# Fourteen modulation parts in each round of the recurrence, none in the output stage and the first norm, and length spreads from rounded halves

## The chip, the cores and the metric

The kernel runs as one program on one core of a Trainium2 chip. A core has TensorE (PE: matmuls, with its weight loads shown as PEld), VectorE (DVE), ScalarE (ACT), GpSimd (POOL) and SyncE (SP, which here only issues DMAs). Each engine works through its own queue in order; semaphores order the queues against each other. The metric is the time of one execution on the device in microseconds (us); smaller is better. Starts of instructions are counted from the beginning of the profiled span.

## The reference

Two blocks are computed one after the other in fp32 for 256 tokens x and 256 context tokens, width 1024. The first is a mixing layer with a gated delta rule in both directions and a pooling branch, the second two layers of feed-forward, mixer (short convolution, then latent attention) and feed-forward. Every norm is scaled and shifted by vectors that a large matrix makes of a condition, the modulation:

```python
def adaln_chunks(cond, w_mod, b_mod):
    m = jax.nn.silu(cond) @ w_mod + b_mod          # [1, 9*D] for each layer
    return jnp.split(m[:, None, :], N_MOD, axis=-1)

# first block
q, k = _l2_norm(q), _l2_norm(k)                    # of 8 heads, 128 wide
o_f, s_f = _gated_delta_rule(q, k, v, g[0], beta[0], s0_f)        # chunks of 64 tokens, forward
o_b, s_b = _gated_delta_rule(flip(q), flip(k), flip(v), ...)      # backward
x = x + gate_x * jnp.einsum('blm,md->bld', y_x, w_out[layer])     # y_x: both mixers, 2048 wide
x = _rms_norm(x, final_gain)
# second block, for x and for ctx
h = h + 0.5 * m[2] * swiglu(rms_norm(h, g) * (1 + m[1]) + m[0])
h = h + m[5] * short_conv_mixer(...) or latent attention
h = h + 0.5 * m[8] * swiglu(...)
```

## The kernel before, in words

**Stages.** The kernel goes through an input stage (0 to about 256 us), the recurrence (256 to about 512), the output stage (to 579), and then the second block: feed-forward 0, short convolution (from about 995), feed-forward 1 and 2, latent attention and feed-forward 3. It is one long queue for TensorE with the other engines around it.

**Dense products.** A weight arrives as a chunk of 128 x 1024 fp32 (`w_raw`, issued by SP). ACT rounds it to fp32r (`w_hi`, L901), POOL makes the rest (`w_lo`, L584), and TensorE multiplies three times for each tile: low weights by high data (L620), high by high (L621), high by low (L624). POOL's wait is for ACT's `w_hi`, TensorE's for POOL's `w_lo`. Four chunks are in flight.

**Modulation parts.** The modulation matrix is streamed as parts of 512 KB, 16 to a group of 2048 columns. A part costs TensorE four matmuls of 512 columns (`mod_part`, L664), it waits for its DMA, and its buffer goes back to SP when it is done. Two parts side by side are what the slots below call a pair; their products run on different rows of the result. When a group is complete, ACT copies the bank to `mod_row` (`act_mod_copy`, L688), TensorE turns it with four transposes (`mod_turn`, L674), and DVE adds the bias (`dve_mod_bias`). The first part of the next group waits for the copy. Parts of the recurrence live in a ring of six buffers (`RECUR_RING`: three `mod_raw`, three `w_raw` that the dense stages don't need at that time), later ones in a ring of nine (`late`).

**The recurrence.** There are eight rounds (`ROUNDS`: four steps, two halves of the heads), each for both directions. `inverse(r)` inverts a triangular matrix by blocks: `left` (L1679) and `right` (L1690) alternate with copies on ACT and products on DVE, then a level of 32-blocks (L1789, L1791), a level of 64-blocks (L1801) and its last product (L1811). Then come the gram and the sums of the next round (L1595, L1605) and the new values (L1713); the state is updated in L1658. ACT makes the decay of a round (`decay`, L1850 and an exponential, L1854), and the copies of each level (L1866, L1875, L1910 to L1930). DVE makes `first_blocks` and `masked_gram` and the products between levels. `some_mods(r, slot)` puts modulation parts at four places of TensorE's queue in each round: "first" (behind the first `left` and `right`), "half" (between the 32-blocks and L1801), "last" (between L1801 and L1811) and "key" (at the end of the round). A copy or a turn of a group is placed at the slot in which the group ends or the next has begun. Before the first `left` of round 0 TensorE runs filler matmuls, `keep_busy(4)`, 512 columns by two each (L722).

**Lengths of keys and queries.** In the input stage, the squares of q and k are summed, DVE and ACT make of them 128 rows `rk` (64 rows `rq`), one row for a head and a quarter of the tokens, with ACT's square root (L1247, L1248). `spread_lengths` (L1130) spreads a row over 128 partitions by four fp32 matmuls whose weights are a broadcast column of the identity; each compiles to two. There are 12 of these calls (8 for keys, 4 for two query heads each), placed between dense products, and DVE multiplies by the result.

**Output stage and first norm.** The output product goes over 16 chunks; parts stand before chunk tiles 10 and 12 (`LATE_OUT`), behind the product and before the spread of the norm (`LATE_END`), and in the first norm of feed-forward 0 (`LATE_TURNS`). SP's loads for them are interleaved with the chunks. A norm is: square sums (L740), a reciprocal root by DVE and ACT, its spread (L759), and the scaled tokens, whose `n_hi` (L866) the first dense product needs. Group 7's copy stands in `act_ffn`, its turn at the start of the short convolution.

## Time and profile before

| | |
|---|---|
| median of 3 runs | 2247.94 us (2246.88 to 2253.41) |
| profiled execution | 2247.81 us |
| its span in the trace | 2246.0 us |
| TensorE busy | 2192.4 us, 98% |
| VectorE, ScalarE, GpSimd busy | 37%, 35%, 45% |
| granted TensorE clock, mean | 0.995 |
| data read from HBM | 294 MB, 132 GB/s |

The profiled execution lies 1.8 us above its own span, which is what a run has around the first and the last recorded instruction. The profile is read by place: a stage's row on the timeline of an engine gives start, time, line and what it works on, "x8" stands for eight instructions merged in one row (start of the first, time from there to the end of the last), and the brackets at the end of a row give the idle time before it and what ended it. Neighbouring matmuls overlap in the rows, since their ends are modelled; the distance between starts is what an instruction costs TensorE's queue. The mean clock is not 1 because of a few short stretches at half rate.

### The profile page before, as it was taken

How to read it: one execution, taken by the hardware profiler on the slowest of the kernel's cores; microseconds unless marked ns; L12 is line 12 of the kernel's file. 1: busy time of each engine (PE TensorE's matmuls, PEld its weight loads, DVE VectorE, ACT ScalarE, POOL GpSimd, SP SyncE). 2: the span in 40 equal slices, each digit the busy share in tenths (PEclk: the TensorE clock that was granted, in tenths of full speed). 3: DMA queues.
4: the chain of work that ended last, by engine and by line, in shares of the span. 5: the costliest groups of instructions: out<-in, count | busy, mean ns of one | idle time of the engine just before them, and what ended most of it. 6: DMA issues, size and time to landing. Idle time of an engine off the chain costs nothing.

```text
span 2246.0 us, 36868 instructions
## 1 busy us (share of the span) xinstructions
PE 2192.4 (98%) x14756; PEld 1789.6 (80%) x14756; DVE 841.6 (37%) x1512; ACT 780.3 (35%) x1259; POOL 1012.4 (45%) x469
## 2 busy tenths in 40 slices
PE   7999999989999999999999999999999999999999
PEld 5789777768788888878878888887888887759999
DVE  4667566665511311343471131133122113562212
ACT  4445434434422122132232212213222222554444
POOL 0457523245344444434434444443444444306888
PEclk9999999999999999999999999999999999999999
DMA  8335466447353323324324323332433323304566
GB/s 288 103 114 162 169 220 223 170 171 276 119 169 94 94 93 94 97 79 172 94 85 163 100 94 94 94 94 90 163 94 94 94 94 118 124 20 124 186 188 188
DMA packets 90932, 297.56 MB, mean 132 GB/s; under 512 B 8992, under 2 KB 21664, under 8 KB 90400
## 3 DMA queue, kind: packets, MB, share of 16 engines
q1 hardware_dynamic: 90640, 295.05, 40.2%
q8 instruction: 117, 1.92, 0.4%
q10 hardware_dynamic: 144, 0.34, 0.1%
q14 instruction: 31, 0.25, 0.0%
HBM read 294.31 MB, written 1.05 MB: 132 GB/s over the span
## 4 chain that ended last, share of the span: by engine, by line
PE 76%; issue 12%; POOL 6%; DVE 3%; ACT 1%; DMA 1%; SPq 1%; POOLq 0%; DVEq 0%; ACTq 0%
PE bank L620 22%; PE bank L624 22%; PE bank L621 22%; POOL w_lo L584 5%; PE bank L664 2%; PE bank L1679 1%; PE bank L1690 1%; DVE gdn_outer L2048 1%; PE bank L1658 1%; PE bank L1595 1%; DMA first_mods<-in_modstream 1%; PE bank L1130 0%; DVE gdn_outer L2050 0%; PE bank L1702 0%; DMA mod_raw<-in_modstream 0%
## 5 line engine op out<-in xcount | busy, mean ns | idle before, releaser
L584 POOL TENSOR_TENSOR w_lo<-w_raw,w_hi 128x1024 fp32r<-128x1024 f32 x378 | 918.9, 2435 | 1054.7 <-ACT w_hi L901 1054.0
L620 PE MATMUL bank<-n_hi,w_lo 128*128 128x512 f32 (+1 forms) x2220 | 788.8, 355 | 5.2 <-ACT n_hi L974 1.8
L624 PE MATMUL bank<-n_lo,w_hi 128*128 128x512 f32 (+1 forms) x2220 | 781.2, 352 | 0.1
L621 PE MATMUL bank<-n_hi,w_hi 128*128 128x512 f32 (+1 forms) x2220 | 781.1, 352 | 0.0
L901 ACT CAST w_hi<-w_raw 128x1024 fp32r<-128x1024 f32 x382 | 400.3, 1050 | 760.5 <-PE bank L624 737.7
L620 PEld LDWEIGHTS bank<-n_hi,w_lo 128*128 128x128 f32 x2220 | 417.6, 188 | 80.3 <-issue 15.4
L624 PEld LDWEIGHTS bank<-n_lo,w_hi 128*128 128x128 f32 x2220 | 417.5, 188 | 64.6 <-DVE n_lo L806 0.6
L621 PEld LDWEIGHTS bank<-n_hi,w_hi 128*128 128x128 f32 x2220 | 417.7, 188 | 62.7
L2461 DVE TENSOR_TENSOR prod<-silu,bank 128x512 f32<-128x512 f32 (+1 forms) x88 | 54.6, 621 | 709.2 <-PE bank L624 692.8
L620 PE MATMUL bank<-g_hi,w_lo 128*128 128x512 f32 (+1 forms) x768 | 283.2, 369 | 1.4 <-DVE g_lo L2452 1.4
L621 PE MATMUL bank<-g_hi,w_hi 128*128 128x512 f32 (+1 forms) x768 | 282.9, 368 | 0.0
L624 PE MATMUL bank<-g_lo,w_hi 128*128 128x512 f32 (+1 forms) x768 | 282.9, 368 | 0.0
L2420 DVE SCALAR_TENSOR_TENSOR h<-bank,gates,h 128x256 f32<-128x256 f32 x136 | 60.7, 480 | 312.8 <-PE bank L624 312.8
L620 PEld LDWEIGHTS bank<-g_hi,w_lo 128*128 128x128 f32 x768 | 144.0, 188 | 28.9 <-DVE g_lo L2452 1.8
L624 PEld LDWEIGHTS bank<-g_lo,w_hi 128*128 128x128 f32 x768 | 144.0, 188 | 27.3
L621 PEld LDWEIGHTS bank<-g_hi,w_hi 128*128 128x128 f32 x768 | 144.0, 188 | 27.2
L2406 ACT ACTIVATE silu<-bank 128x512 f32<-128x512 f32 (+1 forms) x88 | 48.0, 545 | 288.3 <-PE bank L624 288.3
L2452 DVE TENSOR_TENSOR g_lo<-prod,g_hi 128x512 fp32r<-128x512 f32 (+1 forms) x88 | 84.5, 962 | 1.9 <-ACT g_hi L2396 1.9
L1339 DVE SCALAR_TENSOR_TENSOR conv<-bank,cols,conv 128x508 f32<-128x508 f32 (+3 forms) x96 | 63.0, 659 | 42.3 <-ACT conv L1279 39.7
L1980 POOL TENSOR_TENSOR gdn_t<-gdn_inner,consts 128x256 f32<-128x256 f32 x16 | 11.7, 730 | 137.1 <-DVE gdn_inner L2033 137.1
L881 DVE TENSOR_TENSOR nt<-h 128x512 f32<-128x512 f32 (+1 forms) x56 | 58.6, 1047 | 1.8
L866 ACT ACTIVATE n_hi<-nt,mods 128x256 fp32r<-128x256 f32 x88 | 41.0, 505 | 41.8 <-DVE nt L821 41.8
(395 smaller groups left out, 1868.1 us busy)
## 6 DMA issues: line engine op xcount, KB each, us to landing
w_raw<-in_stream SPq DMA_DIRECT2D x383, 512.0 KB, 3.6
late<-in_modstream SPq DMA_DIRECT2D x56, 512.0 KB, 4.6
mod_raw<-in_modstream SPq DMA_DIRECT2D x48, 512.0 KB, 6.3
w_raw<-in_modstream SPq DMA_DIRECT2D x48, 512.0 KB, 5.4
first_mods<-in_modstream SPq DMA_DIRECT2D x6, 1024.0 KB, 11.6
h<-in_tokens SPq DMA_DIRECT2D x2, 1024.0 KB, 6.2
first_mods<-in_modstream SPq DMA_DIRECT2D x4, 512.0 KB, 8.9
consts<-in_consts SPq DMA_DIRECT2D x1, 1152.0 KB, 5.9
```

What stands on the lines that cost most here:

```text
L584: nc.gpsimd.tensor_tensor(w_lo[:, slot, :], w_raw[:, slot, :], w_hi[:, slot, :].bitcast(F32), ALU.subtract).then_inc(w_lo_ready, 1)
L620: nc.tensor.matmul(out_ap, wl, hi, start=start, stop=False)
L621: nc.tensor.matmul(out_ap, wh, hi, start=False, stop=False)
L624: return nc.tensor.matmul(out_ap, wh, lo, start=False, stop=stop)
L664: last = nc.tensor.matmul(bank[MOD_BANK][32 * j:32 * j + 32, :], cond[:, which, k, :], room[:, jj * 512:(jj + 1) * 512], start=(k == 0), s ...
L881: square = nc.vector.tensor_tensor(nt[:, k % 2, s_], h[:, k, s_], h[:, k, s_], ALU.mult)
L901: nc.scalar.copy(w_hi[:, c % RING, :], w_raw[:, c % RING, :]).then_inc(w_hi_ready, 1)
L1339: ins = nc.vector.scalar_tensor_tensor(acc[:, :, to], src[:, :, of], col(Cols.CONV + ci * CONV + j), acc[:, :, to], ALU.mult, ALU.add)
L2406: nc.scalar.activation(silu[:, f % 2, 0:w], bank[(g0 + g) % BANKS][:, 0:w], ACT.Silu).then_inc(gate_ready, 1)
L2420: last = nc.vector.scalar_tensor_tensor(h[:, d, s_], bank[g % BANKS][:, s_], gates[:, gate, d, c:c + 1], h[:, d, s_], ALU.mult, ALU.add)
L2452: nc.vector.tensor_tensor(g_lo[:, f, 0:w], prod[:, f % 2, 0:w], g_hi[:, f, 0:w].bitcast(F32), ALU.subtract).then_inc(hid_lo, 1)
L2461: nc.vector.tensor_tensor(prod[:, f % 2, 0:w], silu[:, f % 2, 0:w], bank[g % BANKS][:, 0:w], ALU.mult).then_inc(groups_read, 2)
```

## The change

`MOD_ROUND` goes from 12 to 14, with 2, 4, 2 and 6 parts in the slots "first", "half", "last" and "key" in place of 2, 2, 4 and 4. The 16 parts of the output stage and of the first norm are no longer there, nor are SP's loads for them, and group 7 is copied and turned within the recurrence. The place of the other copies and turns follows from the counts. The lengths are spread as a rounded half and a rest in fp32r, from rows that ACT lays out for each quarter (12 operations with a scale of zero or one), with the rest made by POOL in front of chunk `TAIL + 8`; a key spread is two matmuls of 512 columns, a query spread four of 256. The value transposes, gates and rate use the modulation bank and the query sums the other one, so that waits move. ACT passes over the pooled groups without waiting for them, one filler matmul is left of four, and DVE makes the first blocks of the forward direction ahead of the backward gram. Three lines with the same bank exchange are cut here.

```diff
@@ -70,7 +70,7 @@
-MOD_ROUND = 12
+MOD_ROUND = 14
 RECUR_RING, LATE_RING = 6, 9
@@ -81,9 +81,9 @@
-LATE_OUT = {10: 2, 12: 2}
-LATE_END = (4, 4)
-LATE_TURNS = {("ffn", 0): (0, 0, 4, None), ("sc", 0): (4, 2, 2, None), ("ffn", 1): (4, 2, 2, 8), ("ffn", 2): (4, 2, 2, None),
+LATE_OUT = {}
+LATE_END = (0, 0)
+LATE_TURNS = {("ffn", 0): (0, 0, 0, None), ("sc", 0): (4, 2, 2, None), ("ffn", 1): (4, 2, 2, 8), ("ffn", 2): (4, 2, 2, None),
               ("mla", 0): (4, 2, 2, 9)}
@@ -321,6 +321,13 @@
             rq = s2("rq", [2 * 32, P])
+            k_rows = s2("k_rows", [P, 4, P])
+            k_rows_hi = s2("k_rows_hi", [P, 4, P], F32R)
+            k_rows_lo = s2("k_rows_lo", [P, 4, P], F32R)
+            q_rows_hi = s2("q_rows_hi", [2 * 32, 2, P], F32R)
+            q_rows_lo = s2("q_rows_lo", [2 * 32, 2, P], F32R)
+            of_quarter = s2("of_quarter", [P, 4])
+            head_rows = s2("head_rows", [P, 32], F32R)
             decay_rate = s2("decay_rate", [16, 16])
@@ -535,21 +542,8 @@
         sp.wait_ge(d_o, 8)
-        for q in range(7):
-            load_late(sp, q)
-        stream_loads(sp, IN_LOADS + RING, CH_OUT + 12)
-        sp.wait_ge(y_lo_ready, 8)
-        for q in (7, 8):
-            load_late(sp, q)
-        q = LATE_RING
-        for i in range(12, 16):
-            load_late(sp, q)
-            q += 1
-            stream_loads(sp, CH_OUT + i, CH_OUT + i + 1)
-        stream_loads(sp, CH_OUT + 16, CH_FFN[0] + RING)
-        for q in range(q, MOD_PARTS):
-            load_late(sp, q)
-        q = MOD_PARTS
+        stream_loads(sp, IN_LOADS + RING, CH_FFN[0] + RING)
+        q = 0
@@ -596,7 +590,11 @@
             low_half(pool, i, i % RING)
-        low_halves(pool, 2 * RING, N_IN)
+        lengths_at = TAIL + 8
+        assert lengths_at % RING == 0
+        low_halves(pool, 2 * RING, lengths_at)
+        pool_lengths(pool)
+        low_halves(pool, lengths_at, N_IN)
         low_half(pool, N_IN, N_IN % RING)
@@ -1087,13 +1085,13 @@
         for t in range(4):
-            last = nc.tensor.transpose(bank[MISC_BANK][:, t * 64:(t + 1) * 64], gb[:, t * P:(t + 1) * P],
+            last = nc.tensor.transpose(bank[MOD_BANK][:, t * 64:(t + 1) * 64], gb[:, t * P:(t + 1) * P],
                                        C(Const.IDENT, 64)[:, 0:64])
...
         pe.wait_ge(rate_diag, 1)
-        nc.tensor.matmul(bank[MISC_BANK][:, 256:272], C(Const.ONES, 16), decay_rate[:], start=True, stop=True)\
+        nc.tensor.matmul(bank[MOD_BANK][:, 256:272], C(Const.ONES, 16), decay_rate[:], start=True, stop=True)\
             .then_inc(rate_rows, 1)
@@ -1115,21 +1113,28 @@
+    q_rows = act_out[0:2 * 32, 0, 0:2 * P].rearrange("p (t c) -> p t c", t=2)
+
+    def pool_lengths(pool):
+        pool.wait_ge(kq_rstd, 3)
+        nc.gpsimd.tensor_tensor(k_rows_lo[:], k_rows[:], k_rows_hi[:].bitcast(F32), ALU.subtract).then_inc(kq_rstd, 1)
+        nc.gpsimd.tensor_tensor(q_rows_lo[:], q_rows, q_rows_hi[:].bitcast(F32), ALU.subtract).then_inc(kq_rstd, 1)
+
     def spread_lengths(pe, j):
...
         if j == 0:
-            pe.wait_ge(kq_rstd, 1)
+            pe.wait_ge(kq_rstd, 5)
             pe.wait_ge(gb_tok_ready, 1)
...
             pe.wait_ge(kq_scaled, j - 1)
-        for t in range(4):
-            q, head, rows = (t, hd, rk) if kind == "k" else (t % 2, hd + t // 2, rq)
-            n = rows.shape[0]
-            last = nc.tensor.matmul(bank[kq_bank(j)][:, t * P:(t + 1) * P],
-                                    C(Const.IDENT, n)[:, 32 * q + head:32 * q + head + 1].to_broadcast([n, P]),
-                                    rows[:], start=True, stop=True)
+        for e, (hi, lo) in enumerate([(k_rows_hi, k_rows_lo)] if kind == "k" else [(q_rows_hi, q_rows_lo)] * 2):
+            n, width = hi.shape[0], hi.shape[1] * P
+            room = bank[kq_bank(j)][:, e * width:(e + 1) * width]
+            head = head_rows[0:n, hd + e:hd + e + 1].to_broadcast([n, P])
+            nc.tensor.matmul(room, head, hi[:].rearrange("p t c -> p (t c)"), start=True, stop=False)
+            last = nc.tensor.matmul(room, head, lo[:].rearrange("p t c -> p (t c)"), start=False, stop=True)
         last.then_inc(kq_bc, 1)
@@ -1153,17 +1158,17 @@
                 pe.wait_ge(silu_done, ci + 1)
-                if ci == 8:
-                    pe.wait_ge(sums_read, 1)
-                else:
+                if ci > 8:
                     pe.wait_ge(vtok_done, ci - 8)
                 for t in range(4):
-                    last = nc.tensor.transpose(bank[MISC_BANK][:, t * P:(t + 1) * P],
+                    last = nc.tensor.transpose(bank[MOD_BANK][:, t * P:(t + 1) * P],
                                                act_out[:, ci % 2, t * P:(t + 1) * P], C(Const.IDENT))
...
                 pe.wait_ge(tile_sq, ci + 1 if ci < 8 else ci - 7)
-                b = MISC_BANK if ci < 8 else MOD_BANK
+                if ci == 16:
+                    pe.wait_ge(sums_read, 1)
+                b = MISC_BANK
                 tiles = w // P
@@ -1244,8 +1249,16 @@
             act.wait_ge(kq_ms, 2)
-            nc.scalar.activation(rk[:], rk[:], ACT.Sqrt)
+            nc.scalar.activation(rk[:], rk[:], ACT.Sqrt).then_inc(kq_rstd, 1)
             nc.scalar.activation(rq[:], rq[:], ACT.Sqrt).then_inc(kq_rstd, 1)
+            act.wait_ge(kq_rstd, 2)
+            for t in range(4):
+                for room in (k_rows, k_rows_hi):
+                    nc.scalar.activation(room[:, t], rk[:], ACT.Identity, scale=of_quarter[:, t:t + 1])
+            for t in range(2):
+                for room in (q_rows, q_rows_hi):
+                    last = nc.scalar.activation(room[:, t], rq[:], ACT.Identity, scale=of_quarter[0:2 * 32, t:t + 1])
+            last.then_inc(kq_rstd, 1)
@@ -1266,6 +1279,8 @@
             for g in groups:
+                if g >= TAIL and IN_TAIL_GROUPS[g - TAIL][0] == "pool":
+                    continue
                 act.wait_ge(linear_done, done_in(g))
@@ -1292,8 +1307,6 @@
                     continue
-                if kind == "pool":
-                    continue
                 if n and IN_TAIL[n - 1][0] == "u":
@@ -1315,17 +1328,21 @@
         nc.vector.memset(row_sum[:], 0.0).then_inc(pads_clear, 1)
+        ident = C(Const.IDENT)
+        nc.vector.tensor_reduce(of_quarter[:], ident.rearrange("p (t h) -> p t h", t=4), AX_X, ALU.add)
+        step(nc.vector.tensor_reduce(k_rows[:, 0, 0:32], ident.rearrange("p (t h) -> p h t", t=4), AX_X, ALU.add))
+        step(nc.vector.tensor_copy(head_rows[:], k_rows[:, 0, 0:32]))
...
             dve.wait_ge(gb_turned, 1)
-            step(nc.vector.tensor_copy(gb_tok[:].rearrange("p t r -> p (t r)"), bank[MISC_BANK][:, 0:256]))
+            step(nc.vector.tensor_copy(gb_tok[:].rearrange("p t r -> p (t r)"), bank[MOD_BANK][:, 0:256]))
             nc.vector.scalar_tensor_tensor(tot[:], gb_tok[:, :, 0:16], -1.0, gb_tok[:, :, 0:16],
...
             nc.vector.tensor_copy(v_tok[:, :, vi, :],
-                                  bank[MISC_BANK][:].rearrange("p (t d) -> p t d", t=4)).then_inc(vtok_done, 1)
+                                  bank[MOD_BANK][:].rearrange("p (t d) -> p t d", t=4)).then_inc(vtok_done, 1)
@@ -1396,7 +1413,7 @@
             dve.wait_ge(tile_used, 24)
-            nc.vector.tensor_scalar(rq[:], bank[MOD_BANK][0:2 * 32, 0:P], EPS, float(P), ALU.add, ALU.mult)\
+            nc.vector.tensor_scalar(rq[:], bank[MISC_BANK][0:2 * 32, 0:P], EPS, float(P), ALU.add, ALU.mult)\
                 .then_inc(sums_read, 1)
@@ -1498,7 +1515,7 @@
-    MOD_SLOTS = {"first": 2, "half": 2, "last": 4, "key": 4}
+    MOD_SLOTS = {"first": 2, "half": 4, "last": 2, "key": 6}
     mod_copies, mod_turns = {}, {}
@@ -1721,7 +1738,7 @@
                 pe.wait_ge(kq_scaled, len(KQ_ITEMS) - 1)
-                keep_busy(4, MISC_BANK)
+                keep_busy(1, MISC_BANK)
             left(r, 1, FWD)
@@ -2081,9 +2098,9 @@
+        first_blocks(0, FWD)
         masked_gram(dve, 0, BWD)
-        for d in (FWD, BWD):
-            first_blocks(0, d)
+        first_blocks(0, BWD)
         for r, (step_, hg) in enumerate(ROUNDS):
@@ -2388,8 +2405,6 @@
         act_norm(act, i, m, w, LATE_TURNS.get(("ffn", n), (None,))[-1])
-        if n == 0:
-            act_mod_copy(act, RECUR_LAST + 1)
         for half in range(2):
@@ -2476,8 +2491,6 @@
         def before_in(g, k):
-            if g == SC_FIRST and k == 0:
-                mod_turn(pe, RECUR_LAST + 1)
             return operands(g, k)
@@ -2519,8 +2532,6 @@
         dve_norm(dve, "sc", i, m, T)
-        dve_mod_bias(dve, RECUR_LAST + 1)
-        dve.wait_ge(mod_ready, MOD_BLOCKS + RECUR_LAST + 1)
         step(dve_gate(dve, 3))
```

## Rows read from the trace of the kernel before

**Rows 1.** The page, busy time of each engine: us, share of the span, instructions.

```profile
PE 2192.4 (98%) x14756; PEld 1789.6 (80%) x14756; DVE 841.6 (37%) x1512; ACT 780.3 (35%) x1259; POOL 1012.4 (45%) x469
```

**Rows 2.** Timeline of ACT, 180 to 184: start us, us, engine, line, operation.

```profile
182.13 0.29 ACT L1248 ACTIVATE rq<-rq 64x128 f32<-64x128 f32 x1
182.33 1.03 ACT L901 CAST w_hi<-w_raw 128x1024 fp32r<-128x1024 f32 x1
```

**Rows 3.** Timeline of ACT, 248 to 262.

```profile
255.08 1.15 ACT L1850 ACTIVATE gdn_dec<-bank,neg_cum 128x128 f32<-128x128 f32 x4 [4.77 <-PE bank L624]
```

**Rows 4.** Timeline of POOL, 183 to 190.

```profile
183.44 7.11 POOL L584 TENSOR_TENSOR w_lo<-w_raw,w_hi 128x1024 fp32r<-128x1024 f32 x3 [2.23 <-ACT w_hi L901]
```

**Rows 5.** Timeline of PE, 185.4 to 186.2.

```profile
185.99 0.35 PE L620 MATMUL bank<-n_hi,w_lo 128*128 128x256 f32 x1 [0.40 <-POOL w_lo L584]
```

**Rows 6.** Two windows: us; busy PE, PEld, DVE, ACT, POOL; PE clock, DMA share, GB/s.

```profile
1945.00:1948.00 3.00, 0.94 (x6) 0.71 (x5) 2.23 (x1) 1.48 (x3) 3.00 (x2) 1.00 0.25 101
1948.00:1951.00 3.00, 3.00 (x9) 2.31 (x9) 2.76 (x6) 1.70 (x4) 1.46 (x1) 0.52 0.64 209
```

**Rows 7.** Timeline of PE, 232 to 238, a key and a query spread.

```profile
232.72 1.05 PE L1130 MATMUL bank<-rk,consts 128*128 128x128 f32 x8
233.53 0.36 PE L620 MATMUL bank<-n_hi,w_lo 128*128 128x256 f32 x1
...
236.56 1.16 PE L1130 MATMUL bank<-rq,consts 64*128 64x128 f32 x8
237.64 0.39 PE L620 MATMUL bank<-n_hi,w_lo 128*128 128x256 f32 x1
```

**Rows 8.** Timeline of PE, 251.5 to 266, the start of the recurrence.

```profile
251.50 1.05 PE L1595 MATMUL bank<-consts,gb_tok 128*128 128x128 f32 x8
...
257.73 3.70 PE L722 MATMUL bank<-consts 128*128 128x512 f32 x8
```

**Rows 9.** Timeline of PE, 335.9 to 345.4, the second half of a round.

```profile
336.66 0.96 PE L1801 MATMUL bank<-gdn_outer,gdn_a 64*64 64x64 f32 x16 [0.66 <-DVE gdn_outer L2134]
337.55 1.07 PE L664 MATMUL bank<-w_raw,cond 128*32 128x512 f32 x8
...
339.41 0.96 PE L1811 MATMUL bank<-gdn_t,gdn_outer 64*64 64x64 f32 x16
```

**Rows 10.** Timeline of ACT, 333.6 to 341, the copy of a group.

```profile
339.57 0.59 ACT L688 COPY mod_row<-bank 128x512 f32<-128x512 f32 x1 [1.47 <-PE bank L664]
```

**Rows 11.** Timeline of PE, 287.3 to 293.7, and from 375.3 to 382.

```profile
288.39 0.62 PE L664 MATMUL bank<-mod_raw,cond 128*32 128x512 f32 x2
...
292.56 1.06 PE L664 MATMUL bank<-mod_raw,cond 128*32 128x512 f32 x8
...
378.57 0.68 PE L1679 MATMUL bank<-gdn_outer,gdn_inner 64*64 64x64 f32 x16 [1.26 <-ACT v_tok L1875]
```

**Rows 12.** SP's loads of modulation parts (L459), 345.3 to 345.95, and their landing.

```profile
L459 SPq DMA_DIRECT2D w_raw<-in_modstream x1: 425/425/425, 345.8 to 345.8; - x1
...
DMA to landing us min/median/max: 3.7/4.2/4.6
```

**Rows 13.** Timeline of PE, 544.9 to 547, the output stage.

```profile
544.97 0.28 PE L624 MATMUL bank<-n_lo,w_hi 128*128 128x256 f32 x1
...
546.17 0.39 PE L620 MATMUL bank<-n_hi,w_lo 128*128 128x256 f32 x1
```

**Rows 14.** Timeline of PE, 578.9 to 590.2, the first norm.

```profile
579.04 3.64 PE L664 MATMUL bank<-late,cond 128*32 128x512 f32 x16
...
589.81 0.50 PE L620 MATMUL bank<-n_hi,w_lo 128*128 128x512 f32 x1
```

**Rows 15.** Timeline of ACT, 579 to 590, the second square.

```profile
579.99 0.49 ACT L2268 ACTIVATE kT<-h,cols 128x256 f32<-128x256 f32 x1
```

**Rows 16.** Timeline of PE, 606.3 to 607.6, feed-forward 0.

```profile
607.19 0.50 PE L620 MATMUL bank<-n_hi,w_lo 128*128 128x512 f32 x1 [0.31 <-POOL w_lo L584]
```

**Rows 17.** Timeline of PE, 994.9 to 996, start of the short convolution.

```profile
995.23 0.60 PE L674 MATMUL bank<-consts,mod_row 128*128 128x128 f32 x4
```

2 lines of the change are left out of this document (1 added, 1 removed).

## The prediction

> **What bounds the kernel now.** I read four views in this order. The page's busy times say that TensorE is busy for 98% of the span and no other engine for half of it [rows 1], so an edit counts where it adds to or takes from TensorE's own queue, or where TensorE waits. The timeline of PE around each edited line then says whether an instruction starts straight behind the one before it (TensorE's own time) or stands behind an idle time with a releaser. The timelines of ACT and POOL at the same moments say what is late next. The landings of SP's loads, last, say when a modulation part can be used at the earliest. TensorE's clock reads 1.0 almost everywhere; the exceptions matter below.
>
> **The change, part by part.** Times are those of the profiled execution, 2247.8 us beside a span of 2246.0; the median is 0.1 us above it, so sum and median can be compared directly.
>
> (a) *Lengths in the input stage.* ACT gets twelve 128-column operations behind the square root of L1248. The one there is followed 0.20 us later by the next [rows 2]; four of L1850 take 1.15, so 0.29 each [rows 3]. Twelve cost 2.4 to 3.4 us, I take 3.0. Behind them on ACT stands the w_hi of chunk 32 (L901), behind that POOL's w_lo (2.37 each) [rows 4], and TensorE already waits 0.40 us for exactly this chunk at 185.99 [rows 5]. No cover: +3.0. POOL's two subtractions (half and a quarter of the columns of an L584: 1.2 and 0.6) stand in front of chunk 33's low half; chunk 33 is ready 1.8 + 2.4 = 4.2 us after chunk 32, TensorE wants it after some 3.3, which is 24 matmuls and the running sums: +0.85. TensorE is then idle for about 3.4 us in one piece. A comparable hole, busy for 0.94 of 3.00 us, is followed by a granted clock of 0.52, which is 1.2 GHz [rows 6]. Three microseconds of it cost half, 1.5 to 1.7, of which 0.85 only takes the place of the wait for chunk 33: +0.85. (Trainium skill, "TensorE: Matmul & The Clock Gate", Part 1: without activity the array falls back to half rate. This trace agrees, and the rule speaks against the change; without it this part would be 0.85 less.)
>
> (b) *The spreads.* A key spread holds TensorE from 232.72 to 233.53, 0.81 us, a query spread from 236.56 to 237.64, 1.08 [rows 7]. The new form streams 1024 columns of fp32r; 24 matmuls of 256 take 3.03 us in the same rows, 0.12 each, so 1024 columns cost 0.48 to 0.5. For the queries, whose weights have 64 rows, the extra 0.27 may stay. No row has this form, so I bound it: 8 x 0.31 and 4 x (0.1 to 0.6) give 2.8 to 4.9, less what goes where TensorE then waits for DVE's scaling; taken 3.7. (a) and (b) together: 3.0 + 0.85 + 0.85 - 3.7 = **+1.0**. The swap of banks 6 and 7 for values, gates and sums removes waits that nobody feels; DVE's three setup operations lie in an idle time of DVE. Nothing for both.
>
> (c) *Start of the recurrence.* ACT's first decay (L1850) starts at 255.08 after 4.77 us idle, released by the last pooled matmul [rows 3], which the new `continue` no longer awaits. Its input, the sums of L1595, is there at 251.50 + 1.05 = 252.6 [rows 8], so the forward decay comes 2.5 us earlier. Now the order counts: DVE does the forward blocks while the backward gram is still being made. ACT's queue (backward decay, cast, three exponentials, the copy of L1875) then sets the first L1679, some 1.8 us earlier than now. The filler matmuls end at 261.43 [rows 8]; with one instead of four (0.93 each) they end at 258.7 and cover nothing that is late. **-1.8**.
>
> (d) *Two more parts in each round.* Four parts take TensorE from 337.55 to 339.41 [rows 9]: 0.93 a pair. Eight pairs are 7.4 us; one more turned group in the recurrence (L674) 0.6. New group ends now fall in the middle of a slot: parts 47|48 (round 2, "half"), 95|96 and 111|112 (rounds 5 and 6, "key"). There part p waits for ACT's copy, 0.59 [rows 10] and two semaphores, about 0.75 each: 2.25. Sum 10.3. What hides it: in "half", L1801 waits 0.66 for DVE (L2134) [rows 9], in five rounds of steps 1 to 3, and 0.1 in round 4: 3.4; in "last" nothing, the pair taken out there is a full gain, counted in the sum; in "key", L1679 waits 1.26 us in round 3 [rows 11], 0.22 in round 1, and the output stage 0.93: 2.4. Left: **+4.5**. Behind the key slot wait left, right and "first" of the next round, all TensorE's own queue.
>
> (e) *The ring of six.* In the old order the two parts of "first" use buffers freed in "last", 10 us before. With six parts in "key" they use those freed by the first pair of "key". That pair starts at K = 288.39, "first" at 292.56 [rows 11], K + 4.2; with one pair more about K + 5.15. Two loads issued behind such a pair (the second at 345.8, the first 0.4 before it, for K = 344.36 [rows 9]) land after 3.7 and 4.6 us [rows 12], so at K + 4.8 and K + 6.1. The second part is 0.95 late, and as both parts run side by side, the lateness is paid in full. Round borders 0, 1, 2, 3, 4 pay 0.85 to 1.0, borders 5 and 6, stretched by a copy and a turn, some 0.2 each: **+5.0**, bounds 0 (other engines' chain is the later one) and 6.5.
>
> (f) *Output stage.* Between the matmuls at 544.97 and 546.17 two parts cost 1.20 - 0.12 = 1.08 us [rows 13]. Two such places: **-2.2**. Twelve loads less on SP's queue there bring chunks earlier, for which TensorE did not wait. The longer "key" slot of round 7 ends with y_lo: nothing.
>
> (g) *First norm.* Four parts run from 579.04 for 3.64 us, twice their price: the clock is low [rows 14]. ACT's last square ends at 580.48 [rows 15], so the sums come 2.1 us earlier; the second and third four give another 1.3 where they outlast the chain on DVE and ACT. TensorE's first matmul moves from 589.81 [rows 14] to about 586.4. But nothing is left that raises the clock before it: 1.4 to 3.1 us of the dense matmuls' time is lost at half rate, 2.2 taken. TensorE's wait at 607.19 for w_lo [rows 16] goes, as ACT comes 3.6 us earlier (3.0 and the copy). -3.4 - 0.3 + 2.2, rounded down for the slower spreads: **-1.6**, bounds -3.3 and 0.
>
> (h) *Short convolution.* The turn at 995.23 goes [rows 17]: **-0.4**.
>
> Sum: 1.0 - 1.8 + 4.5 + 5.0 - 2.2 - 1.6 - 0.4 = +4.5, so 2252.3 us.
>
> **Rivals.** *The landing costs nothing*: (e) is zero since the chains on DVE and ACT end later than the load. For it: DVE works through first blocks of the other direction at that time. Against it: at 292.56 TensorE starts without idle time. 2247.3 us. *Everything moved is hidden*: (d) and (e) are zero and (g) reaches its bound; 2247.8 + 1.0 - 1.8 - 2.2 - 3.3 - 0.4 = 2241.1 us. Against it: the key slots of rounds 0, 2, 4, 5 and 6 have no gap. *The clock falls in the recurrence (slower)*: place: behind the single filler, where TensorE has 1.2 us idle and then halves of a round with 0.4 us holes; the three fillers taken out covered that. Price: half of each low microsecond; 6.8 us low give +3.4, 15 us +7.5, so 2255.7 to 2259.8, middle 2257.5. It decides once low stretches beyond those in my sum pass 4.5 us. For it: the granted clock after [rows 6]; against it: the whole recurrence now runs at 2.4 GHz with holes up to 1.26 us [rows 11]. (The page's rule named above gives this rival too.) *The change doesn't do what it says*: rounded spreads take as long as before; +3.7, 2256.0 us.
>
> **How the numbers follow.** Forecast 0.44, landing free 0.20, all hidden 0.10, clock 0.22, spreads 0.04. A measurement of this kernel can tell about 0.3%, 6.7 us. "All hidden" is faster: 0.10. Clock, spreads and the upper tenth of the forecast (whose own range is 2248 to 2257) are slower: 0.34. The rest is the same: 0.56. Eight times in ten the time lies between 2244.5 and 2259.5: this leaves out most of "all hidden" and the end of the clock case.
>
> **What the profile after will show.** (a) an idle time of about 3.4 us before L620 near 186, released by POOL, and a low clock behind it. (b) spreads of 0.5 us. (c) L1850 near 253 and L1679 near its place minus 1.8. (d) no idle before L1801 in rounds 2 to 7, ACT's copy releasing a part in mid-slot three times. (e) "DMA" as releaser of L664 in "first", 0.9 us in five rounds. (g) a clock of 0.5 when the first feed-forward begins. I am wrong if the recurrence is not longer by about 8 us, or if the clock falls in it.

## The result, and the profile after

The changed kernel takes 2262.97 us (median of 8 runs, 2257.68 to 2267.29), the kernel before 2247.59 us in the same comparison (8 runs). The ratio is 1.0066, with a 95% interval of [1.0053, 1.0079]: slower by 0.66%, some 15 us, where 4.5 were forecast. The profiled execution has a span of 2261.7 us, 15.7 more than before.

The account is read from the timelines of TensorE. Both kernels run the same dense matmuls in the same order, so the start of one and the same matmul in both traces gives how far the changed kernel is behind at this place. The differences between such places are what each part cost:

| up to | start before | start after | behind | this part | forecast |
|---|---|---|---|---|---|
| the wait behind ACT's rows (a) | 185.99 | 189.82 | +3.84 | +3.8 | +3.85 |
| half rate behind them (a) | 189.45 | 194.84 | +5.39 | +1.6 | +0.85 |
| all spreads (b) | 249.97 | 251.42 | +1.45 | -3.9 | -3.7 |
| first L1679 of the recurrence (c) | 261.82 | 261.14 | -0.67 | -2.1 | -1.8 |
| end of the recurrence (d, e) | 518.82 | 531.15 | +12.32 | +13.0 | +9.5 |
| the first six groups of the output product (f) | 551.57 | 561.60 | +10.03 | -2.3 | -2.2 |
| its seventh group | 560.08 | 575.02 | +14.95 | **+4.9** | 0 |
| half rate behind that | 562.76 | 580.06 | +17.30 | **+2.3** | 0 |
| feed-forward 0, the place of [rows 16] (g) | 607.19 | 624.29 | +17.11 | -0.2 | -1.6 |
| short convolution (h) | 995.59 | 1012.23 | +16.65 | -0.5 | -0.4 |
| last stage | 2230.92 | 2246.46 | +15.54 | -1.1 | 0 |

Behind the short convolution the trace of before has two stretches at half rate, near 1948 [rows 6] and 2050, that this one has not. They are worth 1.7 and 0.5 us; half of that is lost again in small steps behind them, which leaves the 1.1 us of the last line. Such stretches are there in some of the traces below and not in others, without an edit near them.

The page of the changed kernel, where [rows 1] stands (busy us, share, instructions). TensorE is busy 3.3 us longer, the other 12.4 are idle:

```profile
PE 2195.7 (97%) x14686; PEld 1791.0 (79%) x14686; DVE 850.4 (38%) x1515; ACT 784.3 (35%) x1271; POOL 1012.4 (45%) x471
```

**Input stage.** Timelines of PE, ACT and POOL (start us, us, engine, line, operation, idle time before and its releaser), and windows (us; busy PE, PEld, DVE, ACT, POOL; clock, DMA share, GB/s):

```profile
189.82 0.36 PE L618 MATMUL bank<-n_hi,w_lo 128*128 128x256 f32 x1 [4.00 <-POOL w_lo L578]
```

```profile
186.22 1.03 ACT L899 CAST w_hi<-w_raw 128x1024 fp32r<-128x1024 f32 x1
```

```profile
186.00:189.00 3.00, 0.00 (x0) 0.00 (x0) 1.42 (x2) 3.00 (x6) 1.67 (x1) 1.00 0.00 0
189.00:192.00 3.00, 2.18 (x14) 2.21 (x15) 2.73 (x10) 0.41 (x1) 3.00 (x4) 0.81 0.37 96
192.00:195.00 3.00, 3.00 (x19) 3.00 (x18) 2.66 (x3) 2.62 (x5) 3.00 (x2) 0.62 0.20 79
```

Where the wait was 0.40 us [rows 5], it is 4.00: the cast that stood at 182.33 [rows 2] stands at 186.22, behind the twelve operations. The twelve take 3.53 us (0.29 each). TensorE does nothing from 186 to 189, and the clock falls behind that. Chunk 33 has no wait of its own, although POOL's two subtractions stand ahead of its low half.

**Spreads and the recurrence.** Timeline of PE. A key spread is two matmuls 0.22 us apart and holds TensorE for 0.46 us, in place of four fp32 products in 0.81 [rows 7]; a query spread takes 0.66 in place of 1.08. The twelve give 4.5 us, of which two new waits for DVE ahead of spreads take 1.3 (0.87 more than before at 213.93, 0.42 at 239.78). Then the "first" slots of rounds 1 and 2 and the "half" slot of round 2, each with the wait that it has got:

```profile
232.68 0.39 PE L1136 MATMUL bank<-k_rows_hi,head_rows 128*128 128x512 f32 x1
232.90 0.39 PE L1137 MATMUL bank<-k_rows_lo,head_rows 128*128 128x512 f32 x1
...
292.03 1.05 PE L662 MATMUL bank<-mod_raw,cond 128*32 128x512 f32 x4
292.96 1.05 PE L662 MATMUL bank<-w_raw,cond 128*32 128x512 f32 x4
295.23 0.68 PE L1696 MATMUL bank<-gdn_outer,gdn_inner 64*64 64x64 f32 x16 [1.22 <-issue]
...
323.03 1.05 PE L662 MATMUL bank<-w_raw,cond 128*32 128x512 f32 x4
325.49 1.05 PE L662 MATMUL bank<-w_raw,cond 128*32 128x512 f32 x4 [1.40 <-DMA w_raw<-in_modstream]
...
341.29 0.62 PE L662 MATMUL bank<-mod_raw,cond 128*32 128x512 f32 x2 [0.82 <-ACT mod_row L686]
```

In round 1 the two parts run one behind the other (four matmuls each, 0.93 apart) instead of side by side as in [rows 11]. In round 2 the second is 2.46 behind the first. The third row with a bracket is the group end inside a slot.

**Output stage.** DVE's and POOL's timelines, then PE's:

```profile
563.00 2.83 DVE L832 TENSOR_SCALAR gates<-mods 128x16 f32<-128x16 f32 x3
565.87 2.60 DVE L877 TENSOR_TENSOR sq_acc<-h 128x256 f32<-128x256 f32 x1
568.50 0.43 DVE L879 TENSOR_TENSOR nt<-h 128x256 f32<-128x256 f32 x1
568.96 2.48 DVE L884 TENSOR_TENSOR sq_acc<-sq_acc,nt 128x256 f32<-128x256 f32 x1
571.47 2.52 DVE L879 TENSOR_TENSOR nt<-h 128x256 f32<-128x256 f32 x1
574.02 0.42 DVE L884 TENSOR_TENSOR sq_acc<-sq_acc,nt 128x256 f32<-128x256 f32 x1
574.48 2.44 DVE L2335 SCALAR_TENSOR_TENSOR h<-bank,mods,h 128x256 f32<-128x256 f32 x6
```

```profile
565.78 2.40 POOL L578 TENSOR_TENSOR w_lo<-w_raw,w_hi 128x1024 fp32r<-128x1024 f32 x1 [0.40 <-ACT w_hi L899]
568.58 2.58 POOL L578 TENSOR_TENSOR w_lo<-w_raw,w_hi 128x1024 fp32r<-128x1024 f32 x1 [0.40 <-ACT w_hi L899]
571.37 2.34 POOL L578 TENSOR_TENSOR w_lo<-w_raw,w_hi 128x1024 fp32r<-128x1024 f32 x1 [0.21 <-ACT w_hi L899]
```

```profile
575.02 0.58 PE L618 MATMUL bank<-n_hi,w_lo 128*128 128x256 f32 x1 [4.87 <-DVE h L2335]
```

The same operation of DVE (L879, L884) lasts 0.42 us where POOL is idle and 2.5 us where it starts beside a low half, and it ends as the low half ends (568.47 beside 568.18; 571.44 beside 571.16; 573.99 beside 573.71). One or two such operations pass for each low half. The chain of gains (L713), gates (L832) and context squares is therefore late, and behind it stand the six updates of h (L2335), which free the banks that TensorE needs. In the kernel before, the same chain met pauses of POOL, since six late loads stood between the chunks on SP's queue (issued from 546.15 to 554.64): chunks issued at 548.26 and 551.49 landed after 6.8 and 6.1 us, where those of the changed kernel take 3.5 to 3.7. Its timelines of DVE and of POOL:

```profile
554.56 0.42 DVE L881 TENSOR_TENSOR nt<-h 128x256 f32<-128x256 f32 x1
555.02 0.42 DVE L886 TENSOR_TENSOR sq_acc<-sq_acc,nt 128x256 f32<-128x256 f32 x1
```

```profile
556.18 4.95 POOL L584 TENSOR_TENSOR w_lo<-w_raw,w_hi 128x1024 fp32r<-128x1024 f32 x2 [1.94 <-ACT w_hi L901]
```

The two places with parts had been cover as well: before, DVE stood idle for 2.24 us ahead of its updates of h (at 558.61), and the parts that are gone are 2.2 us of TensorE's time. e2 below puts the loads back and not the parts, and 0.62 of the 4.87 us are left.

The Trainium skill, page "SBUF — State Buffer", section "Who interferes with whom", states this rule: a VectorE instruction with two SBUF inputs and a GpSimd instruction that reads SBUF share one read interface, and the later one waits for the other's end. The rows agree with it: two SBUF inputs take 2.5 us, L2335 with an input from PSUM 0.41 each (below, also beside a busy POOL).

**First norm.** Windows as above, the second from the first dense matmul on:

```profile
593.65:604.69 11.04, 9.00 (x40) 8.37 (x40) 3.87 (x12) 3.17 (x7) 2.34 (x1) 0.50 0.27 88
...
604.69:610.70 6.01, 6.01 (x14) 4.75 (x15) 5.91 (x15) 2.73 (x6) 0.00 (x0) 0.50 0.00 0
```

The granted clock is 0.50 of full speed, 1.2 GHz, from 593.6 on, for nearly the whole norm and the first 6.0 us of dense work. The kernel before had half rate here too, but from 576.0 to 582.8, and what was left of its parts and of the norm behind that ran at full rate. The spread of the norm shows the difference (timelines of PE, after and before):

```profile
600.14 3.35 PE L757 MATMUL bank<-consts,rstd 128*128 128x128 f32 x12 [0.76 <-ACT rstd L2288]
```

```profile
586.42 1.60 PE L759 MATMUL bank<-consts,rstd 128*128 128x128 f32 x12
```

### The profile page after: what moved, and what is told of

It reads as the page before. It is cut to its first block, busy times and chain, and to the rows that moved or that the text cites. A ratio compares the mean times of both kernels' runs of the same rounds, so it can differ in the third digit from the quotient of the medians.

```text
span 2261.7 us, 36763 instructions
## 1 busy us (share of the span) xinstructions
PE 2195.7 (97%) x14686; PEld 1791.0 (79%) x14686; DVE 850.4 (38%) x1515; ACT 784.3 (35%) x1271; POOL 1012.4 (45%) x471
## 3 DMA queue, kind: packets, MB, share of 16 engines
q8 instruction: 117, 1.92, 0.3%
HBM read 294.31 MB, written 1.05 MB: 131 GB/s over the span
## 4 chain that ended last, share of the span: by engine, by line
PE 77%; issue 10%; POOL 5%; DVE 4%; DMA 2%; ACT 1%; SPq 0%; POOLq 0%; DVEq 0%; ACTq 0%
PE bank L618 22%; PE bank L622 22%; PE bank L619 22%; POOL w_lo L578 5%; PE bank L662 3%; PE bank L1696 1%; DMA w_raw<-in_modstream 1%; PE bank L1707 1%; PE bank L738 1%; DVE gdn_outer L2065 1%; PE bank L1675 0%; PE bank L1612 0%; PE bank L1719 0%; DMA w_raw<-in_stream 0%; DMA first_mods<-in_modstream 0%
## 5 line engine op out<-in xcount | busy, mean ns | idle before, releaser
L879 DVE TENSOR_TENSOR nt<-h 128x512 f32<-128x512 f32 (+1 forms) x56 | 59.1, 1056 | 1.8
```

The source lines that it names most:

```text
L879: square = nc.vector.tensor_tensor(nt[:, k % 2, s_], h[:, k, s_], h[:, k, s_], ALU.mult)
```

## The experiments

Each is compared with the kernel before on the same chip, so the ratios are what stands side by side; places are read in the trace of each run. e1, e2, e3, e5, e6 and e9 start from the changed kernel, e4, e7 and e10 from the kernel before; e8 and e11 are the changed kernel with its moved parts undone.

**e1, context squares behind the updates of h** (changed kernel)

```diff
-    CTX_FIRST = 3
+    CTX_FIRST = 0
```

> The changed kernel with one constant altered: in the output stage DVE makes no context squares ahead of its first six updates of h (CTX_FIRST 0 in place of 3); all of them come behind. In the changed kernel TensorE stands 4.87 us at 570 because the banks are freed by those updates, which begin only at 574.48 behind DVE operations of 2.5 us each. Theory A (DVE's own queue is late, since its operations run in turns with POOL's low halves): the wait of 4.87 us falls below 1.5 us and the low clock behind it (2.2 us) goes: about -6 us, 2257. Theory B (TensorE waits for the chunk that landed at 575.00, 0.02 us before it started): the wait stays, 2263.

Measured: ratio 1.0052 [1.0035, 1.0068]. DVE's updates start at 568.18, 2.73 us after DVE ran dry, and TensorE has no idle time at this place at all:

```profile
568.18 2.45 DVE L2335 SCALAR_TENSOR_TENSOR h<-bank,mods,h 128x256 f32<-128x256 f32 x6 [2.73 <-PE bank L622]
```

Against the trace of the changed kernel, the place of 575.02 comes 5.4 us earlier and that of 579.88 7.7 us earlier; at the place of [rows 16] 7.2 us are left. The spans differ by 5.9, since this trace has the two late stretches at half rate (from 1957.7 and 2060.1) that the one of the changed kernel has not. The wait was DVE's own queue, not the chunk. The timed ratio moved by 0.0014, some 3 us, with an interval of the same size: the place is settled by the trace, the total only to within that.

**e2, nine loads back in the output stage** (changed kernel, no part computed there)

```diff
-        stream_loads(sp, IN_LOADS + RING, CH_FFN[0] + RING)
-        q = 0
+        for q in range(3):
+            load_late(sp, q)
+        stream_loads(sp, IN_LOADS + RING, CH_OUT + 12)
+        sp.wait_ge(y_lo_ready, 8)
+        for q in (3, 4):
+            load_late(sp, q)
...
```

Four more stand ahead of the chunks 12 to 15, as before the change; the nine are not issued again later.

> The changed kernel, with nine of the late modulation loads issued again in the output stage where the kernel before had its own (three ahead of the stage, six between the chunks); they are used later, in the short convolution, and no part is computed in the output stage. Theory A: the loads make the weight chunks late, POOL pauses for 1 us and more two or three times as in the kernel before, DVE's short operations pass in these pauses, the updates of h start at least 3 us earlier and the wait of 4.87 us shrinks to under 2: -3 to -6 us, about 2258. Theory B (the wait is only a matter of the order on DVE or of the shorter output stage, loads don't matter): unchanged, 2263.

Measured: ratio 1.0057 [1.0040, 1.0074], span 2253.8. The wait of 4.87 us is 0.62. The three timelines, DVE, POOL and PE:

```profile
564.87 0.43 DVE L889 TENSOR_TENSOR sq_acc<-h 128x256 f32<-128x256 f32 x1
565.33 0.42 DVE L891 TENSOR_TENSOR nt<-h 128x256 f32<-128x256 f32 x1
...
566.70 2.51 DVE L896 TENSOR_TENSOR sq_acc<-sq_acc,nt 128x256 f32<-128x256 f32 x1
569.24 2.44 DVE L2347 SCALAR_TENSOR_TENSOR h<-bank,mods,h 128x256 f32<-128x256 f32 x6
```

```profile
566.40 5.04 POOL L590 TENSOR_TENSOR w_lo<-w_raw,w_hi 128x1024 fp32r<-128x1024 f32 x2 [2.02 <-ACT w_hi L911]
```

```profile
569.78 0.39 PE L630 MATMUL bank<-n_hi,w_lo 128*128 128x256 f32 x1 [0.62 <-DVE h L2347]
```

Nothing of DVE's order was altered. POOL's pause of 2.02 us, made by a late chunk, let four operations pass at 0.42. The six updates read a bank and run at 0.41 each beside POOL's busy stretch. The timed ratio moved by 0.0009 only, less than its interval; as in e1, the place is settled by the trace (span 7.9 us shorter) and not by the time. So the loads that the change took out had been of use by being in the way.

**e3 and e6, other orders of 14 parts** (changed kernel)

```diff
-    MOD_SLOTS = {"first": 2, "half": 4, "last": 2, "key": 6}
+    MOD_SLOTS = {"first": 2, "half": 4, "last": 4, "key": 4}
```

and for e6, whose round 0 has an order of its own:

```diff
-    MOD_SLOTS = {"first": 2, "half": 4, "last": 2, "key": 6}
+    MOD_SLOTS = {"first": 4, "half": 2, "last": 4, "key": 4}
+    MOD_SLOTS_0 = {"first": 2, "half": 4, "last": 4, "key": 4}
```

> The changed kernel with the 14 parts a round as 2, 4, 4 and 4 (first, half, last, key) in place of 2, 4, 2 and 6. Theory A (with six parts in key and a ring of six, first and the end of key use buffers freed moments ago, and each lateness is paid, 7.3 us in the changed kernel outside of round 0): no wait for DMA in first and key of rounds 1 to 6, the waits hidden behind the longer key slot come back (1.5 us): about -5 us, 2258. Theory B (the memory is the limit, the ring only moves the waits): DMA waits appear in half and last instead, 2262 to 2264.

> The changed kernel with its 14 parts in rounds 1 to 7 as 4, 2, 4, 4 (round 0: 2, 4, 4, 4). Theory A (what costs is how recently the buffer of a part, that of the sixth part before it, was freed: under about 5 us it is late): in this order only the third and fourth part of first are near, and 5 us away; DMA waits outside of round 0 fall from 7.3 to below 2 us; the 0.66 us in front of the 64-blocks' matmul come back in five rounds (+3.1), and so do 1.5 us behind key: net -1 to -3 us, 2256 to 2260 beside 2260 for the changed kernel on the scale of the first comparison. Theory B (the loads of 14 parts don't come in fast enough, wherever they are used): DMA waits of 6 us or more remain.

Measured: e3 1.0123 [1.0106, 1.0140], e6 1.0104 [1.0083, 1.0125], both clearly slower than the changed kernel, where I had expected both faster. Timeline of PE, e3 in the last round and e6 in round 2:

```profile
525.64 1.05 PE L662 MATMUL bank<-w_raw,cond 128*32 128x512 f32 x4 [0.73 <-DMA w_raw<-in_modstream]
528.91 1.92 PE L662 MATMUL bank<-w_raw,cond 128*32 128x512 f32 x4 [2.22 <-DMA w_raw<-in_modstream]
```

```profile
325.61 1.05 PE L662 MATMUL bank<-mod_raw,cond 128*32 128x512 f32 x4 [0.90 <-DMA mod_raw<-in_modstream]
326.86 1.05 PE L662 MATMUL bank<-mod_raw,cond 128*32 128x512 f32 x4 [0.20 <-DMA mod_raw<-in_modstream]
```

For each slot I took its length from the first part to the next other matmul, less 0.465 us a part and 0.58 a turn. What is left over, copies, landings and waits behind the slot together:

| kernel | first, rounds 1 to 7 | half and last, rounds 1 to 7 | key, all rounds | sum of all |
|---|---|---|---|---|
| before | 0.5 | 0.7 | 2.8 | 6.5 |
| changed | 7.2 | 1.6 | 3.9 | 15.5 |
| e3 | 1.8 | 14.5 | 3.4 | 24.6 |
| e6 | 7.0 | 1.6 | 3.6 | 16.1 |

In e3, 5.1 of the 14.5 us fall in the last round. There TensorE waits 0.73 and 2.22 us for loads, and the clock falls: the granted clock is 0.78 from 524 to 531 and 0.54 from 531 to 535, and the second row above takes 1.92 us in place of 1.05.

In e3 the lateness left "first" and came back, more than doubled, in "last": with "half" and "last" four each, the last two parts there use the buffers of the first pair of "half", whose loads were issued at 310.75 in round 1, for instance, and landed at 316.02, when TensorE stood waiting. In e6 the third and fourth part of "first" use those of the first pair of "key"; I had allowed 5 us and called it enough, and they land 5.6 and 6.4 us after their issue (320.00 to 325.56, 320.37 to 326.81), since loads in a burst land one every 1.27 us. On top, the wait ahead of the 64-blocks' matmul (L1801 of the kernel before) is back with 3.86 us in six rounds, as expected (+3.1), which makes most of the 6.1 us by which e6's recurrence is longer. By their recorded signs both runs speak for theory B: in e3 the waits appear in "last", and in e6 about 6 us of landings outside of round 0 remain, where A said below 2. The rate alone does not explain it, though: fourteen landings 1.27 us apart are some 18 us (an estimate), and a round of the changed kernel lasts 34 us on average, with the DMA engines busy for 52 to 66% of it. What the rows show is the weak form of theory A (a buffer freed a few us before its next use makes a part late, the more so as some loads land later than 1.27 us behind the one before); whether an order exists in which 14 parts and six buffers don't meet this stays open. A ring of seven was not tried.

**e4, 12 parts as 2, 4, 2, 4** (kernel before)

```diff
-    MOD_SLOTS = {"first": 2, "half": 2, "last": 4, "key": 4}
+    MOD_SLOTS = {"first": 2, "half": 4, "last": 2, "key": 4}
```

> The kernel before with its 12 parts a round as 2, 4, 2 and 4 in place of 2, 2, 4 and 4, nothing else. My accounting says that the pair moved from last to half hides the 0.66 us of TensorE in front of the 64-blocks' matmul in five rounds, and that last loses nothing: -3 us, less 0.7 for group ends that fall inside a slot: about -2.3 us, 2245.3. Rival (TensorE's waits there are replaced by waits for ACT or DVE one step later): no change, 2247.6.

Measured: ratio 0.9998 [0.9987, 1.0009], no difference. In the trace the last L1811 of the recurrence comes 1.4 us earlier (509.15, 507.73), and so does the output product, where 2.3 were forecast. None of the five waits ahead of the 64-blocks' matmul (3.2 us) is left, but two group ends fall inside "half" and take 1.0 us each, where 0.7 was allowed for both. This is too small for the timing.

**e5, three edits at three places** (changed kernel)

```diff
-            mods_copied(r, "first")
             keep_gram(r, BWD)
+            mods_copied(r, "first")
...
-    CTX_FIRST = 3
+    CTX_FIRST = 0
...
-IDLE = {("ffn", 3): (0, 1, 1)}
+IDLE = {("ffn", 0): (0, 1, 1), ("ffn", 3): (0, 1, 1)}
```

> The changed kernel with three edits at places that don't touch each other, each read at its own place in the trace. (1) Round 1: ACT copies the finished modulation group behind the backward gram instead of ahead of it. If the 1.22 us in front of the backward left of round 1 is this order on ACT, they shrink to below 0.3; if it is the late part itself, they stay. (2) Context squares behind the updates of h, as in e1_squares_later: -4.9 us and the low clock behind them. (3) One filler matmul ahead of the norm's spread and one behind it in the first norm. If the 17 us of low clock from the first norm into feed-forward 0 come from the idle TensorE there, the stretch is shorter by 3 us or more and the first dense matmuls lose less than the 2.7 us of the changed kernel, at a price of 0.5 to 2 us; if the clock follows something else, the stretch stays and the fillers cost 0.5 to 2. Sum against the changed kernel: -7 to -9 us.

Measured: ratio 1.0044 [1.0028, 1.0059], some 5 us under the changed kernel where 7 to 9 were expected; the span, 2253.1, is 8.6 us shorter. Timeline of PE, round 1 and the norm:

```profile
293.24 1.05 PE L662 MATMUL bank<-w_raw,cond 128*32 128x512 f32 x4
294.22 0.68 PE L1696 MATMUL bank<-gdn_outer,gdn_inner 64*64 64x64 f32 x16
...
592.19 1.91 PE L720 MATMUL bank<-consts 128*128 128x512 f32 x2
...
595.60 1.06 PE L720 MATMUL bank<-consts 128*128 128x512 f32 x2
597.01 0.47 PE L618 MATMUL bank<-n_hi,w_lo 128*128 128x512 f32 x1 [0.35 <-ACT n_hi L864]
```

(1) The wait of 1.22 us is gone: it was ACT's order. (2) As in e1. (3) The low clock lasts 10.2 us instead of 17.1 and ends before the dense work, which saves 2.2 us there; the fillers cost 1.5. But e2, with no filler, also shows a stretch of 10.2 us, so it isn't shown that the fillers shortened it.

**e7, the start alone** (kernel before)

```diff
-                keep_busy(4, MISC_BANK)
+                keep_busy(1, MISC_BANK)
...
+        first_blocks(0, FWD)
         masked_gram(dve, 0, BWD)
-        for d in (FWD, BWD):
-            first_blocks(0, d)
+        first_blocks(0, BWD)
...
+                if g >= TAIL and IN_TAIL_GROUPS[g - TAIL][0] == "pool":
+                    continue
                 act.wait_ge(linear_done, done_in(g))
```

> The kernel before with the start of the recurrence alone: one filler, DVE's forward first blocks ahead of the backward gram, ACT not waiting for pooled groups. My step said -1.8 us; in the changed kernel the same place gained 2.1 us although its first parts waited 0.9 us for their DMA. Theory: -2 to -3 us at the first left of the recurrence, kept to the end, 2242.5. Rival (the low clock of TensorE in the recurrence without the fillers): a granted clock of 0.5 near 260 and no gain.

Measured: ratio 0.9997 [0.9988, 1.0007]. In the trace the gain is there and most of it is kept: the first L1679 is at 259.87 (-1.94), the end of the recurrence at 517.43 (-1.39), and the output product keeps the 1.39 up to 562.76.

```profile
257.90 1.13 PE L722 MATMUL bank<-consts 128*128 128x512 f32 x2
259.87 0.68 PE L1679 MATMUL bank<-gdn_outer,gdn_inner 64*64 64x64 f32 x16 [0.85 <-ACT o_sum L1875]
```

The clock stays at 2.4 GHz throughout the recurrence, here and in the changed kernel, so the rival of a falling clock is out for both. It can fall there: in e3 it did, behind waits for loads of 0.73 and 2.22 us.

**e8 and e11, the spreads with their preparations placed otherwise** (changed kernel with 12 parts a round as 2, 4, 2, 4 and the output stage and first norm as before, so the kernel before with the start of e7, the slots of e4 and the spreads)

```diff
+            if TAIL + 5 <= i < TAIL + 8:
+                length_rows(i - TAIL - 5)
...
-        lengths_at = TAIL + 8
+        lengths_at = TAIL + 11
```

This is e8: `length_rows` makes four of the twelve operations, at each of three chunks. e11 has the first two calls there, the third ahead of `u_high`, and keeps `TAIL + 8`:

```diff
+            if TAIL + 5 <= i < TAIL + 7:
+                length_rows(i - TAIL - 5)
...
+                    if n == 6:
+                        length_rows(2)
                     u_high(IN_TAIL[n - 1][1])
```

> Twelve parts a round as 2, 4, 2, 4 with the output stage and the first norm as before, the new start of the recurrence, and the rounded spreads with ACT's twelve operations split over three chunks and POOL's two subtractions three chunks later. If the stall of 3.84 us at 186 in the changed kernel is the queue of ACT and POOL ahead of chunk 32, it is below 1 here and the spreads' gain of about 3.5 us remains: with -2.5 for the start and -1 for the slots 2238 to 2240 beside 2245 before. If the stall has another cause, it stays at this place or moves three chunks on: 2242 to 2244.

> As e10_start_slots, with the rounded spreads; ACT lays out the keys' rows in two chunks and the queries' in its idle time ahead of u_high, POOL subtracts at its old place, ahead of chunk 33, where it is idle for 1 us. In e8_best_of_parts the spreads were worth -3.5 us at their places and 4.8 us were lost at 189 to 206 to POOL's subtractions, to DVE behind POOL and to the clock. If POOL's idle microsecond takes half of the subtractions, at most 1 us of that loss is left: 2.5 us under e10_start_slots, 2239. If POOL is busy without a gap behind any place, the loss comes back behind chunk 33 and the two are equal.

Measured: e8 0.9978 [0.9969, 0.9988], e11 0.9988 [0.9979, 0.9997]. Timeline of PE, e8 three rows, then e11:

```profile
185.86 0.36 PE L631 MATMUL bank<-n_hi,w_lo 128*128 128x256 f32 x1 [0.40 <-POOL w_lo L591]
...
200.66 0.36 PE L631 MATMUL bank<-n_hi,w_lo 128*128 128x256 f32 x1 [0.80 <-POOL w_lo L591]
...
205.55 0.49 PE L1149 MATMUL bank<-k_rows_hi,head_rows 128*128 128x512 f32 x1 [1.85 <-DVE e_tail L1433]
```

```profile
194.37 0.36 PE L631 MATMUL bank<-n_hi,w_lo 128*128 128x256 f32 x1 [3.29 <-POOL w_lo L591]
```

```profile
189.79 1.27 POOL L1133 TENSOR_TENSOR k_rows_lo<-k_rows,k_rows_hi 128x512 fp32r<-128x512 f32 x1 [3.29 <-ACT q_rows_hi L1277]
```

In e8 the stall at 186 is back to its old 0.40: it was ACT's queue, as step (a) said. But 0.4 and 0.8 us appear where POOL subtracts, 1.85 where DVE comes late beside a POOL without pauses, and 1.4 for the clock: 5.1 us behind at 204.87, of which the spreads from there on win back 4.3. The time is between the two forecasts, and the ratio is that of e10, which has the same start and slots without the spreads: they net nothing. In e11 POOL, which works in order, stands 3.29 us for the queries' rows with the chunks behind it. Its forecast (2.5 us under e10) failed: it takes 2243.00 us beside e10's 2241.87. Behind all spreads, at 249.97 of the kernel before, e8 is 0.8 us late, the changed kernel 1.5 and e11 2.5; no placing that was tried made the spreads pay.

**e9, the moved parts undone** (changed kernel; `MOD_ROUND`, slots, `LATE_*`, SP's loads and group 7 as before)

```diff
-MOD_ROUND = 14
+MOD_ROUND = 12
...
-    MOD_SLOTS = {"first": 2, "half": 4, "last": 2, "key": 6}
+    MOD_SLOTS = {"first": 2, "half": 2, "last": 4, "key": 4}
...
```

> The changed kernel with its modulation parts undone: 12 a round as 2, 2, 4, 4, the output stage, the first norm, SP's loads there and group 7 as in the kernel before; spreads, ACT's rows, POOL's place, the bank swap and the start of the recurrence stay as changed. If the loss sits in the moved parts (recurrence 13 us, output stage 4.9, first norm and its clock), this kernel is at +1.45 from the input stage less 2 to 3 for the start: within 2 us of the kernel before, 2243 to 2246. If the new start or the spreads harm the later stages, it stays over 2250.

Measured: ratio 0.9992 [0.9983, 1.0001]. The forecast (within 2 us of the kernel before) held. All of the loss sits in the moved parts: 1.0066 - 0.9992 = 0.0074, 16.6 us.

**e10, start and slots together** (kernel before with e4 and e7)

> The kernel before with the new start of the recurrence and 12 parts as 2, 4, 2, 4, nothing of the spreads. The two edits showed -1.9 and -2.0 us in the traces of their own runs at the end of the recurrence. They are at different places: about -4 us, 2241.5. If the start's gain is only moved to a wait in round 0 (where parts wait for their loads), -2, 2243.5.

Measured: ratio 0.9980 [0.9971, 0.9989], 2241.87 us beside 2246.18. The two together can be told from no change: this version is faster than both kernels. The size is the forecast's, but its source is only half shown. In the traces of e7 and e4 each edit is worth 1.4 us at the end of the recurrence, not 1.9 and 2.0, and here the two are worth 2.2 at that place. The rest of the 4.3 us lies behind it. The trace of before is at half rate from 576.0 to 582.8, those of e7 and e9 for 3.4 us there, and the four with slots 2, 4, 2, 4 (e4, e8, e10, e11) not at all. Whether the edit does this is not shown.

## Why the prediction was wrong

**(a) too small by 0.7 us, its first wait right by luck; (b) and (c) right.** The first wait added 3.84 us beside 3.85, but that figure was 3.0 for ACT's operations and 0.85 for a wait at chunk 33. ACT's twelve took 3.53, outside the 2.4 to 3.4 allowed, and chunk 33 brought no wait. So nothing offset the half rate, which cost 1.6 beside the 0.85 left of it in the sum. The spreads gave 3.9 beside 3.7, the start 2.1 beside 1.8. The spreads lay between their bounds (2.8 to 4.9), near the value taken.

**(d) too small by 1.7 us.** The eight pairs cost 6.9, not 7.4, since a pair behind another one in a slot takes 0.86; the turn cost 0.6 as said, and the waits hidden were 3.2 and 2.4, close to 3.4 and 2.4. Group ends inside a slot cost 1.0 each (from 339.40 to 341.29, less the 0.86 of a pair), not 0.75: +0.8. The step missed is the one that only looked at TensorE's side of a copy: the copy of group 1 now falls in "first", where on ACT it stands ahead of the backward gram, and TensorE waits another 1.22 us (e5 takes that away). The change moves copies past other work on ACT, and I had placed them but not read what they pass.

**(e) right in "first" as a sum, about 2 us missed in "key".** The "first" slots of rounds 1 to 7 wait for landings 0.9, 2.4, 0, 1.1, 0.7, 0.2 and 0 us, 5.4 together beside 5.0. That the sum fits is in part luck, since the forecast had 0.85 to 1.0 in each of the first five: the 2.4 us of round 2 come from a load that landed 3.4 us behind the one before, where 1.3 was reckoned, and round 3 waited for none. The last pair of "key" also uses buffers freed shortly before, in "last", and is 0.6 and 1.5 us late in rounds 1 and 2. Round 0 came out 0.6 us better. (d) and (e) together measured 13.0 in place of 9.5; the pieces named here add up to 13.1. The rivals "landing free" and "all hidden" are out by the same rows.

**(f) is the step that failed.** The two places gave -2.3 as forecast. But the loads taken out were costed at nothing (twelve in its words; SP had issued thirteen from 519.30 to 554.64 and three more in the norm), with the words that the chunks come earlier, "for which TensorE did not wait". True, and the wrong engine: what mattered was POOL's pauses, in which DVE did its short operations. DVE's queue had no slack left, TensorE waits 4.87 us for it (e1 and e2 each take nearly all of that away), and 2.3 more follow at half rate. That is 7.2 of the 11 us missed. The rows for it were in the trace of before: the same DVE operation at 0.42 and at 2.5 us. An average of 37% for DVE [rows 1] hid a stage in which its queue has no slack.

**(g) mis-sized.** TensorE's first dense matmul came 2.4 us nearer (17.30 behind to 14.88), not 3.4: nearly the whole norm, its spread included (3.35 us in place of 1.60), ran at half rate and not only the dense work behind it. That work lost 2.7, in place of 2.2, and the wait for `w_lo` [rows 16] gave 0.5. Net -0.2, inside the bounds of -3.3 and 0, at their end.

**The range** ended at 2259.5, below the 2262.97 measured. It took in the clock in the recurrence, which did not fall, and had no rival in which another engine than TensorE was late in the output stage.

## What to carry to other kernels

A transfer or a filler that is taken away takes its side effects with it: ask of each engine, not of the bound one alone, what it did in the pauses that the transfer made. Where VectorE and GpSimd work at the same time, read VectorE's durations for one and the same operation in a stage; two values far apart, as 0.42 and 2.5 us here, mean that its queue moves at the pace of GpSimd's instructions, and its share of busy time tells nothing. With a ring of buffers, count from the release of a buffer to its next use in the new order, and add at least 1.3 us for each load of 512 KB that is issued in the same burst.

## What the runs showed of the hardware

A DVE operation with both inputs in SBUF (128x256, fp32) takes 0.42 us, and 2.5 us where it begins beside a low half on POOL; one with an input in PSUM takes 0.41 in both cases. Loads of 512 KB issued together mostly landed 1.2 to 1.3 us apart, the first after 3.5 to 3.7 us. In the recurrence of the changed kernel about one in six landed 2.2 to 3.4 us behind the one before (322.02 and 325.44 in round 2), there with the DMA engines 91% busy, and why is open. One modulation part alone occupies TensorE for as long as two side by side, 0.93 us (292.03 to 292.96 for one, 337.55 to 339.41 for two pairs), so a part that is late by 0.9 us costs its lateness in full.
